# Head 0's four column tiles multiplied together, by quarters of x

## The reference

```python
h = _rmsnorm(x, norm_mix_w)          # x: 288 x 2048
proj = h @ w_in                      # w_in: 2048 x 12320 columns
g_qkv, g_z, g_a, g_b, m_qkv, m_i, m_f, m_o, gate_a, gate_b = split(proj)
c, new_gdn_conv = _causal_dwconv(g_qkv, gdn_conv_buf, gdn_conv_w); c = silu(c)
gq, gk = l2norm(heads of c) ...; g = -exp(A_log) * softplus(g_a + dt_bias); beta = sigmoid(g_b)
go = gated delta rule over chunks of gq, gk, gv, g, beta     # 8 heads of 128
mh = chunked mLSTM of m_qkv, m_i, m_f                        # 8 heads of 128
x = x + (sigmoid(gate_a) * (go' @ w_branch_a) + sigmoid(gate_b) * (mh' @ w_branch_b)) @ w_out
h = _rmsnorm(x, norm_ffn_w); u = dwconv(h @ w_up); x = x + (silu(u_gate) * u_val) @ w_down
```

## Time and profile before

| | |
|---|---|
| median of 3 runs | 1892.6 us (1892.35 to 1895.57) |
| profiled execution, its own time | 1893.78 us |
| its span in the trace | 1892.0 us |
| PE busy | 1877.0 us, 99% of the span |
| PE weight load busy | 1844.5 us, 97% |
| DVE, ACT, POOL busy | 1226.8, 918.6, 158.4 us |
| moved by DMA | 308.26 MB, mean 163 GB/s |
| mean granted TensorE clock | 0.999 of full speed |

### The profile page before, as it was taken

The page is one execution under the profiler, slowest core; times in us unless marked ns, Lnnn a source line. Parts: engine busy times, 40 slices in busy tenths (PEclk is TensorE's granted clock), DMA queues, the critical chain, the costliest instruction groups (busy, mean ns, idle before and its releaser), DMA issues.

```text
span 1892.0 us, 38581 instructions
## 1 busy us (share of the span) xinstructions
PE 1877.0 (99%) x14270; PEld 1844.5 (97%) x14270; DVE 1226.8 (65%) x2623; ACT 918.6 (49%) x1803; POOL 158.4 (8%) x327
## 2 busy tenths in 40 slices
PE   9999999999999999999999999999999999999999
PEld 8899999999999999999999999999999999999998
DVE  5877777777746566666655666754567764466753
ACT  5554455554544444555545445444444444354554
POOL 4000010100100011000021000000000000000022
PEclk9999999999999999999999999999999999999999
DMA  8546556565557675646775566666566566656462
GB/s 226 154 126 167 135 156 167 142 163 139 145 154 185 179 190 157 180 149 188 193 189 149 158 180 164 170 171 168 154 162 179 158 168 167 171 147 178 133 172 86
DMA packets 572817, 308.26 MB, mean 163 GB/s; under 512 B 10607, under 2 KB 567815, under 8 KB 572695
## 3 DMA queue, kind: packets, MB, share of 16 engines
q1 hardware_dynamic: 531571, 281.24, 55.0%
q10 hardware_dynamic: 41124, 25.39, 4.8%
HBM read 293.58 MB, written 13.02 MB: 162 GB/s over the span
## 4 chain that ended last, share of the span: by engine, by line
PE 95%; DVE 3%; ACT 1%; issue 0%; DMA 0%; SPq 0%; ACTq 0%; DVEq 0%
PE products L1849 29%; PE products L1851 28%; PE products L1850 28%; PE mixer L1830 2%; PE mixer L1949 1%; DVE w_lo L606 1%; PE mixer L1957 1%; ACT w_hi L599 0%; PE products L2021 0%; DVE S_sample L1584 0%; PE mixer L2051 0%; PE products L2287 0%; DMA x_s_rows<-in_x_sample 0%; PE products L2015 0%; PE mixer L1927 0%
## 5 line engine op out<-in xcount | busy, mean ns | idle before, releaser
L606 DVE TENSOR_TENSOR w_lo<-w_raw,w_hi 128x512 fp32r<-128x512 f32 x1037 | 719.3, 709 | 573.0 <-ACT w_hi L599 570.8
L599 ACT ACTIVATE w_hi<-w_raw 128x512 fp32r<-128x512 f32 x1037 | 629.3, 626 | 586.2 <-PE products L1851 564.8
L1849 PE MATMUL products<-h_hi,w_hi 128*128 128x288 f32 x1536 | 476.6, 310 | 0.1
L1850 PE MATMUL products<-h_lo,w_hi 128*128 128x288 f32 x1536 | 453.8, 295 | 0.0
L1851 PE MATMUL products<-h_hi,w_lo 128*128 128x288 f32 x1536 | 453.1, 295 | 0.0
L1849 PE MATMUL products<-f_hi,w_hi 128*128 128x288 f32 x1408 | 417.0, 296 | 0.0
L1850 PE MATMUL products<-f_lo,w_hi 128*128 128x288 f32 x1408 | 415.4, 295 | 0.0
L1851 PE MATMUL products<-f_hi,w_lo 128*128 128x288 f32 x1408 | 414.5, 294 | 0.0
L1849 PEld LDWEIGHTS products<-h_hi,w_hi 128*128 128x128 f32 x1536 | 289.3, 188 | 13.7 <-issue 9.2
L1850 PEld LDWEIGHTS products<-h_lo,w_hi 128*128 128x128 f32 x1536 | 289.7, 189 | 0.4
L1851 PEld LDWEIGHTS products<-h_hi,w_lo 128*128 128x128 f32 x1536 | 289.5, 188 | 0.0
(11 more groups left out here) (465 smaller groups left out, 2210.9 us busy)
## 6 DMA issues: line engine op xcount, KB each, us to landing
w_raw<-in_w_in SPq DMA_DIRECT2D x95, 1024.0 KB, 6.0
w_raw<-in_w_up SPq DMA_DIRECT2D x88, 1024.0 KB, 5.8
w_raw<-in_w_down SPq DMA_DIRECT2D x32, 1024.0 KB, 5.9
w_raw<-in_w_out SPq DMA_DIRECT2D x16, 1024.0 KB, 7.1
w_raw<-in_w_down SPq DMA_DIRECT2D x16, 768.0 KB, 5.0
w_raw<-in_w_branch_a SPq DMA_DIRECT2D x8, 1024.0 KB, 5.7
w_raw<-in_w_branch_b SPq DMA_DIRECT2D x8, 1024.0 KB, 5.8
S_sample<-in_state_gdn_S ACTq DMA_DIRECT2D x8, 512.0 KB, 6.1
```

What stands on the lines that cost most here:

```text
L599: nc.scalar.activation(ring_slot(whi, whi2, n, ring), raw[:, s % slots, 4 * j:4 * j + 4], ACT.Copy).then_inc(hi_ready, 1)
L606: nc.vector.tensor_tensor(ring_slot(wlo, wlo2, n, ring), raw[:, s % slots, 4 * j:4 * j + 4], ring_slot(whi, whi2, n, ring).bitcast(F32), A ...
L1849: mm(out, w_hi, x_hi, start=start, stop=False)
L1850: mm(out, w_hi, x_lo, start=False, stop=False)
```

## The change

Six things change.

1. Slots 0 to 15 go through head 0's quad by quarters: slot n is quarter n // 4 of x and column tile n % 4 (`front_tile`). The four column tiles fill their four PSUM banks side by side, and are complete after slots 12 to 15.
2. The weights of that quad come in 16 pieces of a quarter of a column tile each. Column tile 0 of the next quad comes in four pieces too, each when its place in `w_raw` is free.
3. The sample rows are loaded once, into `xs4`, four DMAs on ACT's queue instead of eight on SP's. `x_rows` has two parts.
4. `turn_x` handles a pair of tiles: two transposes of 32 rows from `xs4`, then four of 128. Tiles 0 to 3 are turned before slot 0 and the pairs 4, 6, 8, 10, 12, 14 before slots 1, 2, 5, 6, 9, 10. From tile 4 on only two PSUM banks are used, so a pair waits for the lower parts of the pair ahead. The third and fourth bank take the constants and the small products.
5. `evacuate(0)` to `(3)` run at slots 13 to 16. The matmuls for `r_tok` stand before the small product of slot 11 instead of that of slot 9.
6. `WARM` is 9, and `PREP_AT[0]` is 18; the other heads stay where they were.

On SP's queue the nine DMAs of the rows of constants stand ahead of the last column group of x and of the weights of quarters 2 and 3. The diff, cut to its core:

```diff
-WARM = 14
-PREP_AT = [17 + 28 * h for h in range(8)]
+WARM = 9
+PREP_AT = [18] + [17 + 28 * h for h in range(1, 8)]
...
-        x_rows = nc.alloc_sbuf_tensor_at("x_rows", [P, 3, D], F32, offset=b_zm)
+        x_rows = nc.alloc_sbuf_tensor_at("x_rows", [P, 2, D], F32, offset=b_zm)
...
-            for g in range(4):
+            def x_piece(g):
                 cc = slice(g * NG, (g + 1) * NG)
                 sp.dma_start(x_rows[:, 0:2, cc], xp_rows[:, :, cc]).then_inc(x_in[g], 16)
-                sp.dma_start(raw[:, 0, 4 * g:4 * g + 4], w_in[:, 4 * g:4 * g + 4, 0:P]).then_inc(first_in[g] if g < 3 else landed[0], 16)
-                sp.dma_start(x_rows[0:TS, 2, cc], xs_rows[:, cc]).then_inc(x_in[g], 16)
-                sp.dma_start(xs4[:, g], xs_rows[:, cc].rearrange("t (m p) -> m t p", p=P)).then_inc(x_in[g], 16)
-            unit(w_in, 0, KT, columns("g", 0, 1), 0, 1, first=True)
-            unit(w_in, 0, KT, columns("g", 0, 2), 0, 2, first=True)
+
+            def w_pieces(g, *tiles_):
+                for s in tiles_:
+                    sp.dma_start(raw[:, s, 4 * g:4 * g + 4], w_in[:, 4 * g:4 * g + 4, bass.ds(columns("g", 0, s), P)])\
+                        .then_inc(first_in[g][s] if g < 3 else landed[s], 16)
+
+            x_piece(0)
+            w_pieces(0, 0, 1)
+            x_piece(1)
+            w_pieces(0, 2, 3)
+            w_pieces(1, 0, 1)
+            x_piece(2)
+            w_pieces(1, 2, 3)
...
+            x_piece(3)
+            w_pieces(2, 0, 1)
...
-            unit(w_in, 0, KT, columns("g", 0, 3), 0, 3, first=True)
+            w_pieces(2, 2, 3)
+            w_pieces(3, 0, 1, 2, 3)
...
-                    if q:
+                    if q == 1 and s == 0:
+                        for g in range(4):
+                            sp.wait_ge(lo_ready, 4 * g + 1)
+                            sp.dma_start(raw[:, 0, 4 * g:4 * g + 4], w_in[:, 4 * g:4 * g + 4, bass.ds(columns(kind, i, 0), P)])\
+                                .then_inc(next_in[g] if g < 3 else landed[0], 16)
+                    elif q == 1:
+                        sp.wait_ge(lo_ready, 13 + s)
+                        unit(w_in, 0, KT, columns(kind, i, s), q, s, first=True)
+                    elif q:
                         unit(w_in, 0, KT, columns(kind, i, s), q, s)
...
+        def front_tile(n):
+
+            return (n % 4, n // 4) if n < 16 else (n // 4, n % 4)
+
+        def front_hi(n):
+            t, j = front_tile(n)
+            s = t % 4
+            if n < 12:
+                nc.scalar.wait_ge(first_in[j][s], 16)
+            elif 16 <= n < 19:
+                nc.scalar.wait_ge(next_in[j], 16)
+            else:
+                nc.scalar.wait_ge(landed[s], 16 * (t // 4 + 1))
+            if n >= 4:
+                nc.scalar.wait_ge(blocks, n - 3)
+            nc.scalar.activation(whi[:, n % 4], raw[:, s, 4 * j:4 * j + 4], ACT.Copy).then_inc(hi_ready, 1)
+
+        def front_lo(n):
+            t, j = front_tile(n)
+            nc.vector.wait_ge(hi_ready, n + 1)
+            nc.vector.tensor_tensor(wlo[:, n % 4], raw[:, t % 4, 4 * j:4 * j + 4], whi[:, n % 4].bitcast(F32), ALU.subtract).then_inc(lo_ready, 1)
...
+        def x_bank(f):
+
+            return f if f < 4 else f % 2
+
+        def x_tiles(work):
+            for g in range(1, 4):
+                for h in range(2):
+                    yield 4 * g - 3 + h
+                    work(4 * g + 2 * h)
...
+            for g in range(4):
+                act.dma_start(xs4[:, g], xs_rows[:, g * NG:(g + 1) * NG].rearrange("t (m p) -> m t p", p=P)).then_inc(x_in[g], 16)
+                if g == 0:
+                    act.dma_start(norm_rows[:], a["norm_mix_w"][0].rearrange("(k p) -> k p", p=P)).then_inc(norm_in, 16)
...
+            def x_upper(f):
                 act.wait_ge(*st_t.after(f"x{f}"))
-                nc.scalar.activation(h_hi[:, f], pm[:, f % 4, 0:T], ACT.Copy, scale=wn[:, 0, f:f + 1])\
+                nc.scalar.activation(h_hi[:, f], pm[:, x_bank(f), 0:T], ACT.Copy, scale=wn[:, 0, f:f + 1])\
                     .then_inc(*st_a.done(f"hi{f}"))
-                if f % 4 == 3 and f < 15:
-                    act.wait_ge(first_in[f // 4], 16)
-                    nc.scalar.activation(whi[:, f // 4], raw[:, 0, f - 3:f + 1], ACT.Copy).then_inc(hi_ready, 1)
+
+            for f in range(4):
+                x_upper(f)
+                if f % 2:
+                    front_hi(f // 2)
+            front_hi(2)
...
-                dve.wait_ge(blocks, 4 * (t + 1))
+                dve.wait_ge(blocks, t + 13 if t < 4 else 4 * (t + 1))
...
-                split_lo(0, slot + 3, 4)
-
-                if slot == 12:
-                    evacuate(0)
-                    evacuate(1)
-                if slot >= 12 and slot % 4 == 0:
+                if slot + 3 < SLOTS:
+                    front_lo(slot + 3)
+                else:
+                    split_lo(0, slot + 3, 4)
+
+                if 13 <= slot < 17:
+                    evacuate(slot - 13)
+                elif slot >= 20 and slot % 4 == 0:
                     evacuate(slot // 4 - 1)
...
                 if f % 4 == 0:
-                    pe.wait_ge(x_in[f // 4], 48)
+                    pe.wait_ge(x_in[f // 4], 32)
                 if f >= 4:
-                    pe.wait_ge(*st_d.after(f"lo{f - 4}"))
-                for n, t0, c in PARTS:
-                    last = turn(pm[:, f % 4, t0:t0 + n], x_rows[0:n, c, f * P:(f + 1) * P], n)
-                last.then_inc(*st_t.done(f"x{f}"))
+                    pe.wait_ge(*st_d.after(f"lo{f - 3 if f < 6 else f - 1}"))
+                for f_ in (f, f + 1):
+                    own = slice(f_ % 4 * TS, (f_ % 4 + 1) * TS)
+                    nc.tensor.transpose(pm[:, x_bank(f_), TP:T], xs4[own, f // 4], ident[own, own])
+                for f_ in (f, f + 1):
+                    for n, t0, c in PARTS[:2]:
+                        last = turn(pm[:, x_bank(f_), t0:t0 + n], x_rows[:, c, f_ * P:(f_ + 1) * P], n)
+                    last.then_inc(*st_t.done(f"x{f_}"))
...
+                    if b == 2:
+                        pe.wait_ge(*st_d.after("diag"))
+                        for c in range(2):
+                            mm(pm[:, 2, c * P:(c + 1) * P], ones[:], diag[:, c], start=True, stop=True)
+                        for m in range(4):
+                            last = mm(pm[:, 2, TP:T], ones[:], diag[:, 2, m * TS:(m + 1) * TS], start=m == 0, stop=m == 3)
+                        last.then_inc(*st_t.done("r"))
...
-                t, j = slot // 4, slot % 4
+                t, j = front_tile(slot)
                 if j == 0:
-                    pe.wait_ge(bank_free, t + 3 if t >= 4 else 4)
+                    pe.wait_ge(bank_free, t + 3 if t >= 6 else t + 1 if t >= 4 else 4)
                 pe.wait_ge(lo_ready, slot + 1)
-                if t == 0:
-                    pe.wait_ge(*st_d.after(f"lo{4 * j + 3}"))
                 for k in range(4):
                     kk = 4 * j + k
-                    last = product(front_bank(t), whi[:, j, k], wlo[:, j, k], h_hi[:, kk], h_lo[:, kk], kk == 0, kk == KT - 1)
+                    if t == 0 and (j == 0 or k == 0):
+                        pe.wait_ge(*st_d.after(f"lo{kk if j == 0 else 4 * j + 3}"))
+                    last = product(front_bank(t), whi[:, slot % 4, k], wlo[:, slot % 4, k], h_hi[:, kk], h_lo[:, kk], kk == 0, kk == KT - 1)
                 last.then_inc(blocks, 1)
 
-            front(pe, weights, [Lane(0, gates_rows())] + [Lane(PREP_AT[h], prepare(h)) for h in range(H)]
+            turn_x(0)
+            turn_x(2)
```

More of the change, by code:

```diff
@@ L888, in gates_rows, with small_upper @@
                                          accum_out=ss_part[:, 0, g:g + 1]).then_inc(*st_a.done(f"sq{g}"))
-                    act.wait_ge(*st_a.after(f"sq{g}"))
+                def small_upper(b):
+                    act.wait_ge(small_in, 32)
+                    nc.scalar.activation(small_of(sm_hi, b), small_from(b), ACT.Copy).then_inc(*st_a.done(f"smhi{b}"))
+                for g in range(3):
+                    yield 3 + 2 * g
+                    square(g)
+                yield 8
+                small_upper(0)
@@ L902, in gates_rows @@
+                yield 10
+                small_upper(2)
+                yield 11
+                small_upper(3)
+                act.wait_ge(consts, 1)
+                act.wait_ge(*st_t.after("r"))
+                nc.scalar.activation(r_tok[:], pm[:, 2, 0:T], ACT.Ln, bias=eps[:], scale=1.0 / D).then_inc(*st_a.done("rln"))
+                act.wait_ge(*st_a.after("rln"))
+                nc.scalar.activation(r_tok[:], r_tok[:], ACT.Exp, scale=-0.5).then_inc(*st_a.done("rexp"))
                 yield 13
@@ L1336, in gates_rows @@
                    ALU.mult).then_inc(*st_d.done("diag"))
[L1337 to L1341 removed]
+                small_lower(2)
+                yield 11
+                small_lower(3)
                 yield 13
```

115 lines of the change are left out of this document (55 added, 60 removed).

## The result

The changed kernel takes 1897.01 us (median of 20 runs, 1896.34 to 1899.71). The kernel before took 1894.02 us beside it (median of 20 runs, 1892.27 to 1897.71). The medians differ by 3.0 us. The ratio is 1.0020, with a 95% interval of 1.0014 to 1.0026, which is 3.8 us (2.7 to 4.9): the change makes the kernel slower. The executions of the changed kernel fall into two groups, 12 at 1896.34 to 1897.04 and 8 at 1898.88 to 1899.71; the profiled one belongs to the first, and what the second group loses beside it is not shown. The forecast was no change, 1892.0 us, with a range up to 1895.0. (Its yardstick was the 1892.6 us of three runs; against that, the upper end allowed a loss of 2.4 us.) The profiled execution took 1897.04 us for a span of 1895.3, against 1893.78 and 1892.0 before: 3.3 us more in both.

What follows compares the result with a forecast made beforehand. PE was taken as the bound, busy 1877.0 of 1892.0 us. The terms to slot 45 summed to 0.0, a median of 1892.6, put at 1892.0 because unlikely ends lean to gain; range 1888.2 to 1895.0.

Steps and rivals of the forecast that it cites:

- Start: Up to the first product: it comes at 9.35 us against 12.76, tiles 4 to 7 still unturned; +1.2 us (0 to +1.8).
- the early start is not had: Rival at the start: shared bandwidth holds the first product until 10.6, time 1893.3; counted within the 0.66 for no change.
- Turns in pairs: PE's turns before slots 0 to 10: more switches cost 0.5 us, overlapping 32-row transposes return 0.5; 0 (-0.5 to +0.9).
- Waits inside the first 16 slots: PE's 0.8 us wait for the diagonal goes, 0 to 0.5 remains for lower parts of tile pairs; +0.6 us (0 to +1.0).
- Clock: At the start, over slot 0: one stretch at 1.2 GHz again; 0, or +1.3 us without one.
- DMA order: SP's queue: constants ahead of quarter 2's weights, which land near 21 us, wanted about 20.9; -0.5 us (0 to -1.7).
- Slots 13 to 27: DVE is the limit; evacuations among the gate chain delay evacuate(3) and `sq_lo`; -1.0 us (-1.7 to +1.7).
- Slots 27 to 45: DVE's level pieces meet evacuations on even slots, while two `x_xt` waits lose their cause; -0.3 us (-1.2 to +1.0).
- The slot later pays: Rival, slots 13 to 27: DVE's queue is not the limit, +1.7 instead of -1.0, time 1888.1; chance 0.24 with its kin.
- The clock stays low: Rival, slots 0 to 6: three more stretches at 1.2 GHz cost 3.9 us, time 1896; 0.10 with other DVE queue slips.

Runs made afterwards that it cites:

- e1: The changed kernel with the norm rows' load issued ahead of the sample rows on ACT's queue: 1899.93 us, 1.0032 of the kernel before.
- e2: e1 plus x's last column group and the first two weight pieces of quarter 2 ahead of the constants on SP's queue: 1893.62 us, 0.9996 of the kernel before.
- e7: e2 with ACT's piece of the gate rows moved from slot 35 to 36: 1892.96 us, 0.9991 of the kernel before.
- e10: e8 with the gate chain's pieces of slots 15, 16 and 18 one slot later: 1893.29 us, 0.9996 of the kernel before.
- e5: The changed kernel with only SP's order edited, x's last group and two quarter 2 weight pieces ahead of the constants: 1894.52 us, 0.9996 of the kernel before.
- e4: The kernel before with only head 0's preparation moved from slot 17 to 18: 1895.45 us, 1.0011 of the kernel before.
- e8: e2 with head 0's preparation back at slot 17: 1893.60 us, 0.9991 of the kernel before.
- e9: e7 with the gate chain's pieces of slots 15, 16 and 18 one slot later: 1893.40 us, 0.9996 of the kernel before.
- e3: The changed kernel with head 0's preparation back at slot 17: 1898.17 us, 1.0020 of the kernel before.
- e6: e2 with the old warm-up, WARM 14 instead of 9: 1893.83 us, 0.9994 of the kernel before.
- e12: e5 with the norm rows' load on SP's queue between the first two weight pieces: 1894.65 us, 1.0000 of the kernel before.
- e11: The kernel before with only head 0's evacuations moved to one each at slots 13 to 16: 1895.71 us, 1.0007 of the kernel before.

## Why the prediction was wrong

The working is on record above; this goes through its terms. The sum to slot 45 was 0.0 and measured −2.9 (117.30 to 120.20).

*Start: +1.2 forecast, −1.2 measured (1.0 us earlier, less 2.2 us of turning still to do). This is the step that failed.* PE started 1.0 us earlier with 2.2 us less of turning done. The chain from the first turn to the first product was right, 8.65 to 11.73 = 3.1 us against a forecast 3.25. The turn's own start was wrong, 8.65 instead of 6.1. The prediction put it at the landing of column group 0 and counted the move of four DMAs to ACT's queue as free. It did not follow the norm rows, which every `h_hi` needs. The kernel before asks for them first on ACT's queue, and the change puts them behind a load of sample rows and behind what SP had asked for by then. The load of the norm rows in the kernel before:

```profile
DMA to landing us min/median/max: 2.8/2.8/2.8
```

It took 6.6 us in the changed kernel and 2.8 when it went first again (e1). PE waits 2.4 us for it, of which 1.2 us come back at the first product in e1. The rest lies with the sample rows themselves: with the norm rows first and the new warm-up, PE still waits 0.7 to 1.5 us for them and turns x at 7.2 to 7.9 us (e1, e2, e7 to e10), so 6.1 was also too early by more than a microsecond. The rival "the early start is not had" had this sign and half the size: it put the first product at 10.6, where it came at 11.7. Those six kernels have it at 10.45 to 10.96, about where that rival put it.

*Turns in pairs: 0 forecast, +2.1 measured.* The timeline above shows the two 32-row transposes as one start of 0.25 us, and 0.60 us from the first of the pair to the next product, with 0.08 us ahead of it: 0.68 for two tiles, where two cost 1.1. Five pairs at that price and one at the low clock (about 1.1) make 4.5 us for 12 tiles, which the old price makes 6.6. The gain is twice the upper end that I gave. I had priced the overlap of two 32-row transposes alone. In the trace of the kernel before, a tile's 0.545 us hold 0.20 us from the second 128-row transpose to the 32-row one and 0.18 us from there to the next 128-row one; in pairs each of these changes comes once for two tiles. The rule of the Trainium skill that the prediction set beside this term, "TensorE: Matmul & The Clock Gate", Part 3, a weight load overlaps matmuls that use another row group, agrees with this trace: the two loads start 0.004 us apart and the two matmuls 0.003, so the second load runs while the first matmul does.

*Waits inside the first 16 slots: +0.6 forecast, +0.6 measured.* The 0.8 us for the diagonal are gone, and 0.2 us for a small weight's lower part took their place.

*Clock: 0 forecast, −0.8 measured.* The low stretch was twice as long, 6.83 us, and 1.5 us of it lay ahead of the products. From its first matmul to the next turn, the block of slot 0 took 3.15 us and that of slot 1 2.28; in the kernel before it was 3.05 and 1.60.

*DMA order: −0.5 forecast, −1.5 measured,* near the lower end of 0 to −1.7. The place was right: ACT waits for `w_raw`, and the next pair of tiles stands behind it. The time was not. SP's queue in the changed kernel, first and last of the constants and what follows:

```profile
12.90 1.47 SPq L499 DMA_DIRECT2D w_rows<-in_gdn_conv_w  x1
...
19.45 0.51 SPq L506 DMA_DIRECT2D gdn_norm_w_t<-in_gdn_norm_w  x1
20.01 0.43 SPq L485 DMA_DIRECT2D x_rows<-in_x_prompt  x1
20.49 1.03 SPq L489 DMA_DIRECT2D w_raw<-in_w_in  x2
```

The constants held the queue for 7.1 us, from 12.90 to 19.96, as sized (6.5), but it got to them 2.4 us later than I put it, and the piece landed at 25.3 instead of 21, 4.9 us after its issue where I had put 3. The worth of it is the wait of 1.47 us, which e5 takes away.

The terms to slot 13 are −1.2 + 2.1 + 0.6 − 0.8 − 1.5 = −0.8, and 50.63 − 49.74 is 0.9; a tenth stays unassigned.

*Slots 13 to 27: −1.0 forecast, −0.9 measured.* This step was right in size and in what limits the stretch, and wrong in one of its places. e4 and e8 show that the evacuations cost 1.1 to 1.2 us and the slot gives back 0.1 to 0.25. e9 and e10 bear out that DVE is the limit there. The queue of DVE in the changed kernel, slots 13 to 16, the first of three evacuations, the gates' chain and `z`, which is `evacuate(3)`:

```profile
52.17 0.42 DVE L1500 TENSOR_TENSOR gdn_qkv<-products,r_token 128x256 f32<-128x256 f32 x1
...
57.64 0.45 DVE L1438 SCALAR_TENSOR_TENSOR softplus_rows<-linear_rows,softplus_rows 128x288 f32<-128x288 f32 x1
...
59.74 0.18 DVE L1444 TENSOR_TENSOR e_row<-gdn_rows_sb 8x32 f32<-8x32 f32 x1
...
60.57 0.45 DVE L1523 TENSOR_TENSOR z<-products,r_token 128x288 f32<-128x288 f32 x1
```

`z` starts 9.94 us after slot 13, where it was 58.38 − 49.74 = 8.64 us in the earlier trace rows: 1.3 later for the 0.9 of the forecast. But PE was one slot later too, and the wait for the last columns is 1.1 instead of 1.4. The 2 us or more that I expected at `sq_lo` are 1.07 there and 1.17 ahead of block 25, whose split stands behind pieces of the gate rows in DVE's queue, 70.60 to 72.94 us (timeline of PE in the changed kernel):

```profile
73.72 0.40 PE L1942 MATMUL products<-h_hi,w_hi 128*128 128x288 f32 x1 [1.17 <-DVE w_lo L649]
...
78.23 0.40 PE L2001 MATMUL mixer<-sq_hi,ones 128*128 128x288 f32 x1 [1.07 <-DVE sq_lo L1565]
```

e4 has both, and the kernels with slot 17 (before, e3, e8) have no such wait ahead of block 25, so it came with the later slot.

*Slots 27 to 45: −0.3 forecast, −1.1 measured.* It is a mis-sized term, inside its range (−1.2 to +1.0) at its lower end. The prediction looked at DVE's pieces only. What decided stands on ACT: e4 shows `p_sb` behind the gates' piece, e7 shows 0.8 us of it by moving that piece. In the kernels with slot 18, slots 36, 40 and 44 are 0.5, 0.4 and 0.8 us longer than in the kernel before, with waits of 0.23, 0.16 and 0.45 us for `x_xt` in them, which fits the collisions with evacuations that I named; slot 41 is 0.7 us shorter.

*The rivals.* "The slot later pays" was wrong in its premise: e4 gives 0.13 us where it wanted 1.7. "The clock stays low" had the right sign for a half, two stretches instead of its four. The loss came from four terms that each went the wrong way and one that gained 2.1 us over its forecast. Twenty runs on each side tell 1.1 us from no change, half the width of the interval, where I had allowed 3.8. The range, which I cut to half of the losing ends, was too narrow: it allowed 2.4 us of loss and 3.0 came. Half of those ends is 3.2 us, and I counted it from 1892.0, the sum moved towards the gain; from 1892.6 it would have reached 1895.8, which the measured 1897.01 exceeds too, since the kernel before itself has 1894.02 in twenty runs. That the two large misses, the start and the turns, have opposite signs is luck: without the 2.1 us of the turns the loss would have been near 5.

The new front is not slower by itself: with the norm rows first and the constants behind, it reaches slot 13 by 1.1 to 2.5 us earlier than the kernel before (e2, e7 to e10). It then pays 1.1 to 1.2 us for evacuating four tiles in four slots. No version measured here is faster than the kernel before by more than the interval; the best are e7 and e8 with 0.9991 (0.9982 to 1.0000).

## What to carry to other kernels

When a start is rearranged, list for the first instruction of each engine every load that it needs, the smallest too, and place them ahead of the bulk; 8 KB asked for second instead of first cost 0.4 to 1.2 us of the first product here. Before an early stage is made earlier, look up the absolute time at which the data of the next stage arrive: e1 gained 1.2 us at the start and lost 3.3 us later, since the wait grew and the clock fell with it. Moving a lane by one slot moves it against the queues of all engines, so each engine's order at the new slot is to be read, not only that of the busiest.

## What the runs showed of the hardware

- A load of 8 KB took 2.8 to 3.0 us when asked for first (before, e1, e2, e6 to e10), and 6.6, 6.3 and 5.9 us (after, e5, e12) when others were asked for ahead of it, on either of two queues.
- Two transposes of 32 rows on different row groups start 0.003 us apart (after). A change between 128-row and 32-row transposes cost 0.18 to 0.20 us from start to start (before). A turn of two tiles took 0.68 us arranged so, against 1.1 with 32-row and 128-row transposes by turns.
- The granted clock fell to 0.50 after long waits in the middle of work (after 3.12 us in e1 for 6.83 us, after 2.7 us in e3 and e11 for 3.4 us), but after the same 2.7 us in e8 it did not. What decides there stays open. At slot 27 the stretch of e3 had cost 0.54 us against e8 (29.03 and 28.49), which runs the same instructions from slot 13 on; there DVE is the limit, and part of PE's delay shortens later waits.
- Fronts that have the same instructions up to slot 13 (e2, e7 to e10) reached it at 47.57, 48.42, 48.60, 47.76 and 47.28 us. Differences of this size between single profiles are no evidence on an edit of the start. Where the low stretch lies makes part of them. It ends at 16.4 and 16.9 us in e7 and e8. In e2, e9 and e10 the clock row of the start shows 1.00, but the products start 0.24 us apart until about 14 us, as at 1.2 GHz, so the row misses the stretch there. Two windows of e2 (columns as above) show it in PE's matmuls, 11 and then 17 in 2 us:

```profile
12.00:14.00 2.00, 2.00 (x11) 1.72 (x9) 1.32 (x3) 0.63 (x1) 1.62 (x7) 1.00 1.09 314
14.00:16.00 2.00, 2.00 (x17) 1.94 (x18) 1.33 (x4) 1.41 (x3) 1.59 (x7) 1.00 0.95 240
```
